# A softmax attention stage inside a two-layer encoder: order of rotation, scores, transposes and one vector's column sums

## The reference

```python
qa = partial_rotary(qa.reshape(B, L, DIFF_HEADS, 2, DIFF_QK_DIM), cos, sin)
ka = partial_rotary(ka.reshape(B, L, DIFF_HEADS, 2, DIFF_QK_DIM), cos, sin)
...
s = jnp.einsum('bqhcd,bkhcd->bhcqk', q_blk, k).astype(jnp.float32) * scale
p = jax.nn.softmax(s, axis=-1)
a = p[:, :, 0] - lam * p[:, :, 1]
return jnp.einsum('bhqk,bkhe->bqhe', a.astype(v.dtype), v)
```

## Time and profile before

| | value |
|---|---|
| median of three runs | 2928.39 us |
| runs | 2918.54, 2929.75, 2928.39 us |
| profiled execution: span from first to last instruction | 2927.6 us |
| mean granted TensorE clock over the span | 0.950 |
| PE busy | 2643.3 us (90%) |
| DVE busy | 1887.8 us (64%) |
| ACT busy | 1084.7 us (37%) |
| POOL busy | 131.7 us (4%) |
| HBM read | 613.50 MB |

### The profile page before, as it was taken

How to read it: one execution, slowest core, us unless ns; L and a number is a source line. 1 busy time by engine, 2 the same in 40 slices (tenths; PEclk the granted TensorE clock), 3 DMA queues, 4 the chain that set the end, 5 groups by cost and what they waited for, 6 DMA issues and landing times.

```text
span 2927.6 us, 43304 instructions
## 1 busy us (share of the span) xinstructions
PE 2643.3 (90%) x17226; PEld 2127.0 (73%) x17226; DVE 1887.8 (64%) x1930; ACT 1084.7 (37%) x872; POOL 131.7 (4%) x201
## 2 busy tenths in 40 slices
PE   6969999966778999999999967859979999999997
PEld 3438888832367788888888862548868888888886
DVE  7866666567645776776777757646676666555555
ACT  3333333334423333334444421123333343344442
POOL 1020000000000200000000021010020000000000
PEclk9989999987979999999999978979989999999999
DMA  7988888712423788787877759378837777555551
GB/s 251 346 275 268 282 265 278 242 54 65 145 101 129 244 281 272 258 274 264 281 262 278 278 170 225 131 197 286 298 110 236 238 233 239 187 186 186 175 185 56
DMA packets 289323, 638.99 MB, mean 218 GB/s; under 512 B 78338, under 2 KB 79364, under 8 KB 285636
## 3 DMA queue, kind: packets, MB, share of 16 engines
q1 hardware_dynamic: 239284, 583.70, 60.1%
q0 software_dynamic: 11008, 35.99, 4.2%
q10 hardware_dynamic: 38928, 17.86, 2.3%
HBM read 613.50 MB, written 19.79 MB: 216 GB/s over the span
## 4 chain that ended last, share of the span: by engine, by line
PE 78%; DVE 12%; ACT 4%; ACTq 3%; DMA 1%; issue 1%; SPq 1%; DVEq 0%
PE PS L267 46%; PE PS L268 24%; ACT Pb L967 2%; ACTq L1011 2%; DVE Pb L1747 2%; DVE acc L1742 1%; PE PS L913 1%; PE PS L184 1%; PE PS L719 1%; PE PS L220 1%; DMA omat<-WF 1%; DVE wlo L257 1%; PE PS L740 1%; ACTq L419 1%; ACT HF L967 1%
## 5 line engine op out<-in xcount | busy, mean ns | idle before, releaser
L267 PE MATMUL PS<-H,whi 128*128 128x512 f32 x5888 | 2084.2, 399 | 99.3 <-DVE wlo L257 75.5
L268 PE MATMUL PS<-H,wlo 128*128 128x256 f32 x5888 | 1656.9, 281 | 0.0
L267 PEld LDWEIGHTS PS<-H,whi 128*128 128x128 f32 x5888 | 1112.6, 189 | 371.0 <-DVE wlo L257 81.7
L257 DVE TENSOR_TENSOR wlo<-raw,whi 128x2048 fp32r<-128x2048 f32 x368 | 843.5, 2293 | 740.1 <-ACT whi L253 739.6
L253 ACT ACTIVATE whi<-raw 128x2048 fp32r<-128x2048 f32 x368 | 705.6, 1918 | 1261.0 <-PE PS L268 1227.9
L268 PEld LDWEIGHTS PS<-H,wlo 128*128 128x128 f32 x5888 | 1119.6, 190 | 0.0
L176 DVE SCALAR_TENSOR_TENSOR acc<-araw,cact,acc 128x1024 f32<-128x1024 f32 x240 | 307.1, 1280 | 1.4 <-DMA araw<-in_ada_w 0.8
L967 ACT ACTIVATE Pb<-PS 128x1024 f32 (+5 forms) x117 | 117.9, 1035 | 151.7 <-issue 59.4
L967 ACT ACTIVATE H<-Pb 128x512 fp32r (+2 forms) x142 | 94.8, 668 | 42.6 <-DVE Pb L1414 28.7
L1462 DVE TENSOR_TENSOR H<-Pb,H 128x512 fp32r<-128x512 f32 x128 | 87.6, 685 | 0.0
L1358 DVE TENSOR_TENSOR raw<-Pb,HF 128x1024 f32<-128x1024 f32 x64 | 74.1, 1220 | 9.8 <-DMA omat<-WF 7.0
(11 more groups left out here) (262 smaller groups left out, 1328.7 us busy)
## 6 DMA issues: line engine op xcount, KB each, us to landing
raw<-in_mlp_w SPq DMA_DIRECT2D x256, 1024.0 KB, 6.0
araw<-in_ada_w SPq DMA_DIRECT2D x276, 512.0 KB, 4.6
raw<-in_mix_w_in SPq DMA_DIRECT2D x64, 1024.0 KB, 7.6
raw<-in_s_w_glu SPq DMA_DIRECT2D x32, 1024.0 KB, 7.3
acc<-in_ada_w SPq DMA_DIRECT2D x44, 512.0 KB, 7.2
raw<-in_ada_w POOLq DMA_DIRECT2D x32, 512.0 KB, 4.1
raw<-in_mix_w_out SPq DMA_DIRECT2D x16, 1024.0 KB, 5.2
vmat<-Pb ACTq DMA_DIRECT2D x8, 1024.0 KB, 7.4
```

The costliest lines, as they stand in the source:

```text
L257: nc.vector.tensor_tensor(wlo[:, s % 2, :], raw[:, s, :], whi[:, s % 2, :].bitcast(F), ALU.subtract).then_inc(S("lo_done"), 1)
L267: nc.tensor.matmul(PS[:, b, :], w[0], H2[:, :, k, :], start=first, stop=False, skip_group_check=True)
L268: return nc.tensor.matmul(PS[:, b, 0:T], w[1], H2[:, 0, k, :], start=False, stop=last, skip_group_check=True)
```

## The change

The diff below is complete but for context. In words:

- Rotation groups go in the order 0, 2, 1, 3 (ROT_ORDER). Scores of heads 0 to 3 need groups 0 and 2 alone. DVE does three rotations, then `row_max(0)` and `row_max(1)`, then the fourth rotation.
- On PE the wait for all rotations and all copies ahead of the first scores is replaced by waits for the copies that free their banks (`vt_evac` 6 and 8) and for two rotations (`rot_done` 2, and 3 at turn 8). The wait for four rotations stands after scores 1.
- On ACT the three sigmoids stand ahead of all eight copies.
- `ada_sum(pe, SCALE1, 7)` moves from after scores 1 to decay level 3, behind that level's gate parts, with a wait for `lv_put` 2. `ada_finish` on DVE moves to level 5, ahead of its multiply. The turn of the gate vector at level 6 waits for it.
- GATE_WIN moves to columns 1120 to 1232 of `acc`, away from SCALE1's half.
- In the loop PE computes scores n+2 ahead of the wait for `at_mix` and the transposes.
- The masks get a semaphore of their own (`ld_mask`), and their load waits for SHIFT1 rather than SCALE1.

```diff
--- before.py
+++ after.py
@@ -198,7 +198,7 @@
     AREAS = [acc[:, 1024 * k:1024 * k + 1024] for k in range(4)] + [araw[:, k, :] for k in range(2)]
     ROWS = 3 * D // 512
     GATE_ROWS = D // 512
-    GATE_WIN = acc[:, 3072:3184].rearrange("p (k m) -> p k m", k=16)
+    GATE_WIN = acc[:, 1120:1232].rearrange("p (k m) -> p k m", k=16)
     GATE_TURN = acc[0:GATE_ROWS, 2560:3072]
     GT = acc[0:ROWS, 0:512]
 
@@ -364,6 +364,7 @@
 
 
 
+    ROT_ORDER = (0, 2, 1, 3)
     ROTW = raw[:, 3, 0:128]
     COS = raw[:, 3, 128:384]
     SIN = raw[:, 3, 384:640]
@@ -533,10 +534,10 @@
             load(ROTW, a["rot"], "ld_rot")
             load(COS, a["cos"], "ld_rot")
             load(SIN, a["sin"], "ld_rot")
-            sp.wait_ge(S(f"{SCALE1.name}_freed"), 1)
+            sp.wait_ge(S(f"{SHIFT1.name}_freed"), 1)
             for q in range(4):
                 load(acc[32 * q:32 * q + 32, 640:1120].rearrange("p (m t) -> p m t", m=15),
-                     a["masks"][:, 0:32, 0:32].rearrange("m s t -> s m t"), "ld_rot")
+                     a["masks"][:, 0:32, 0:32].rearrange("m s t -> s m t"), "ld_mask")
             sp.wait_ge(S("gate_used"), 32)
             for s in plan_out:
                 stream(s)
@@ -754,25 +755,27 @@
                                                    Pb[:, (16 if w == 0 else 48) + h, t * P:(t + 1) * P], ident[:])
                     last.then_inc(S("vt_T"), 1)
 
-                for g in range(4):
-                    if g >= 2:
-                        pe.wait_ge(S("rot_done"), g - 1)
+                for i, g in enumerate(ROT_ORDER):
+                    if i >= 2:
+                        pe.wait_ge(S("rot_done"), i - 1)
                     for z in range(2):
                         n = 2 * g + z
-                        last = nc.tensor.matmul(PS[:, 4 + 2 * (g % 2) + z, :], ROTW, PF[:, n * 512:(n + 1) * 512],
+                        last = nc.tensor.matmul(PS[:, 4 + 2 * (i % 2) + z, :], ROTW, PF[:, n * 512:(n + 1) * 512],
                                                 start=True, stop=True)
                     last.then_inc(S("rot_mm"), 1)
-                    values(0, g)
+                    values(0, i)
                 for g in range(4):
                     pe.wait_ge(S("vt_evac"), g + 1)
                     values(1, g)
-                pe.wait_ge(S("rot_done"), 4)
-                pe.wait_ge(S("vt_evac"), 8)
 
                 def scores(n):
                     h, qt = n // 2, n % 2
                     if n >= 2:
                         pe.wait_ge(S("at_exp"), n - 1)
+                    else:
+                        pe.wait_ge(S("vt_evac"), 6 + 2 * n)
+                    if n in (0, 8):
+                        pe.wait_ge(S("rot_done"), 2 + n // 4)
                     for c in range(2):
                         last = nc.tensor.matmul(PS[:, 2 * (n % 2) + c, 0:T],
                                                 Pb[64 * c:64 * c + 64, h, qt * P:(qt + 1) * P],
@@ -781,18 +784,18 @@
 
                 for n in range(2):
                     scores(n)
-                ada_sum(pe, SCALE1, 7)
+                pe.wait_ge(S("rot_done"), 4)
                 pe.wait_ge(S("win_ready"), 2)
                 nc.tensor.matmul(PS[:, 6, 0:2], ones[:, 0:P], ZERO2, start=True, stop=True, skip_group_check=True)
                 for n in range(16):
                     h, par = n // 2, n % 2
+                    if n < 14:
+                        scores(n + 2)
                     pe.wait_ge(S("at_mix"), n + 1)
                     for kt in range(2):
                         last = nc.tensor.transpose(PS[:, 4, par * T + kt * P:par * T + (kt + 1) * P],
                                                    EA[:, par, 0, kt * P:(kt + 1) * P], ident[:])
                     last.then_inc(S("at_T"), 1)
-                    if n < 14:
-                        scores(n + 2)
                     pe.wait_ge(S("at_Te"), n + 1)
                     for kt in range(2):
                         last = nc.tensor.matmul(PS[:, 5, par * T:par * T + P], Vn[:, h, kt, :], AT[:, par, kt, :],
@@ -844,7 +847,11 @@
                     if lv < 7:
                         for c in range(GATE_SPLIT[lv], GATE_SPLIT[lv + 1]):
                             gate_part(pe, c)
+                    if lv == 3:
+                        pe.wait_ge(S("lv_put"), 2)
+                        ada_sum(pe, SCALE1, 7)
                     if lv == 6:
+                        pe.wait_ge(S(f"{SCALE1.name}_freed"), 1)
                         gate_turn(pe)
                 pe.wait_ge(S("sc_ready"), 4)
                 pe.wait_ge(S("lv_put"), 7)
@@ -1098,11 +1105,10 @@
                 run(RS[n - 1], PS[0:ROWS, 0, 0:T], ACT.Sqrt, "rms_std", scale=1.0 / P, bias=eps[0:ROWS, 1:2])
 
             def attention_act():
+                run(PF[:, 8192:12288], PF[:, 8192:12288], ACT.Sigmoid)
+                run(SIGQ, QH, ACT.Sigmoid)
+                run(SIGG, GH, ACT.Sigmoid, "hg_sig")
                 for g in range(8):
-                    if g == 4:
-                        run(PF[:, 8192:12288], PF[:, 8192:12288], ACT.Sigmoid)
-                        run(SIGQ, QH, ACT.Sigmoid)
-                        run(SIGG, GH, ACT.Sigmoid, "hg_sig")
                     act.wait_ge(S("vt_T"), g + 1)
                     dst = (HF[:, 0:2048] if g < 4 else PF[:, 4096:6144])[:, 512 * (g % 4):512 * (g % 4) + 512]
                     run(dst, PS[:, g % 4, :], sem="vt_evac")
@@ -1521,13 +1527,18 @@
             v.wait_ge(S("ld_rot"), 48)
             v.wait_ge(S("in_done"), 1)
             cs, sn = (z.unsqueeze(1).broadcast_to([P, 4, T]) for z in (COS, SIN))
-            for g in range(4):
-                v.wait_ge(S("rot_mm"), g + 1)
+
+            def rotate(i):
+
+                g = ROT_ORDER[i]
+                v.wait_ge(S("rot_mm"), i + 1)
                 qk = Pb[:, 4 * g:4 * g + 4, :]
-                link(tt(ROTT, bank(4 + 2 * (g % 2), 2).rearrange("p (b t) -> p b t", b=4), sn, ALU.mult))
+                link(tt(ROTT, bank(4 + 2 * (i % 2), 2).rearrange("p (b t) -> p b t", b=4), sn, ALU.mult))
                 link(tt(qk, qk, cs, ALU.mult))
                 link(tt(qk, qk, ROTT, ALU.add))
                 v.sem_inc(S("rot_done"), 1)
+            for i in range(3):
+                rotate(i)
 
             def rms_inverse(n):
                 v.wait_ge(S("rms_std"), n)
@@ -1606,12 +1617,12 @@
                     link(tt(LN_KEY[0], LC[0], LN_KEY[0], ALU.subtract))
                 else:
                     link(tt(LN_KEY[1], LC[1], LN_KEY[1], ALU.add))
-                    v.wait_ge(S("ld_rot"), 112)
+                    v.wait_ge(S("ld_mask"), 64)
                     link(tt(acc[:, 640:864], acc[:, 640:864], acc[:, 864:1088], ALU.add))
 
             row_max(0)
             row_max(1)
-            ada_finish(v, link, SCALE1, 7)
+            rotate(3)
             link(nc.vector.memset(TINY, 1e-18))
             link(nc.vector.memset(GATE_WIN, 0.0))
             link(nc.vector.tensor_copy(GATE_WIN[:, :, GATE_ROWS - 1:GATE_ROWS].rearrange("p k m -> p (k m)"), cact[:]))
@@ -1671,6 +1682,8 @@
             for lv in range(1, 8):
                 if lv < 7:
                     level_arg(lv + 1)
+                if lv == 5:
+                    ada_finish(v, link, SCALE1, 7)
                 level_mul(lv)
                 if lv == 1:
                     level_put(1, 0, 0)
```

## The result

The changed kernel takes 2900.8 us (median of 4 runs, 2895.25 to 2905.83) against 2929.07 us (4 runs, 2918.54 to 2934.04): ratio 0.9919, 95% interval 0.9895 to 0.9944. The forecast was 2906.4 us, with a range of 2895 to 2920. The profiled execution took 2899.89 us and has a span of 2897.8 us, so 2.1 us lie around the span, not the 0.8 that I took.

What follows compares the result with a forecast made beforehand. Mostly PE products over the whole span; in this stage a serial chain before the loop, then DVE. Gains of 24.3 us less 0.3 and 2 gave 22: span 2905.6, plus 0.8 makes 2906.4 us, range 2895 to 2920.

Steps and rivals of the forecast that it cites:

- Up to `mix(0)`: Stretch before the loop: `mix(0)` starts at 604.95 instead of 617.24, 12.3 us gained, with the fourth rotation late next.
- Turns 0 and 1: First loop turns: PE's clock falls in the gap, leaving 12.0 us gained so far; 13.6 if the clock stays up.
- Turns 2 to 8: Maxima of scores 3 to 10: seven intervals, three of 4.0 and four of 4.1, 28.5 us in all; 8.2 us gained.
- Logarithms: Turn 8: the waits for ACT's logarithms stay; only the transposes no longer precede scores 12, 0.4 us gained.
- Turns 11 to 14: Late loop, called turns 11 to 13 in the forecast: DVE's full hole goes, 3 x 1.23 = 3.7 us gained.
- Levels: Decay levels: column sums hidden in PE's slack, taken as 0; DVE's addition and handshake cost 0.3 us.
- Clock in the loop: Low-clock stretches of PE in the loop, up to 3 us each for three; taken as a loss of 2 us.
- Rival 1: PE's clock oscillates through the loop, which gains nothing; only 12.3 us before it stay: 2916 us, chance 0.14.

Runs made afterwards that it cites:

- x6: Changed kernel with only ACT's three sigmoids put back behind the fourth copy: median 2911.94 us, ratio 0.9959 to the kernel before.
- x3: Changed kernel with only the scale vector's column sums put back ahead of the loop, in bank 7: median 2911.62 us, ratio 0.9973 to the kernel before.
- x5: Changed kernel with only all four rotations put back ahead of the first scores: median 2900.11 us, ratio 0.9911 to the kernel before.
- x7: Changed kernel plus six useless 128x512 products in PE's gap ahead of the loop: median 2897.79 us, ratio 0.9922 to the kernel before.
- x10: Changed kernel plus useless products in both PE gaps, six ahead of the loop, seven in turn 9: median 2901.34 us, ratio 0.9907 to the kernel before.
- x1: The changed kernel timed again with no edit: median 2897.21 us against 2920.16 for the kernel before, ratio 0.9923.
- x4: Changed kernel with the column sums ahead of the loop in bank 4, free after the third rotation: median 2907.31 us, ratio 0.9947 to the kernel before.

## Why the prediction was right or wrong

- *Up to `mix(0)`:* 12.3 us forecast, 12.2 measured (33.97 - 21.77). The fourth rotation was late next, as forecast. The share of each edit is another than its size suggests. Undone one by one, and counted from DVE's first rotation, the sigmoids are worth 9.0 us, the column sums 7.3, the order of rotations and scores 0. The first two make 16.3 and not 12.2 because each was undone in the new order: there the fourth rotation comes behind the late sigmoids (x6), under which it ran before, and the sums in bank 7 wait for it (x3). With all rotations first, x5 beside the kernel before, the first scores come at 18.04 instead of 23.92 us, and `mix(0)` 3.53 instead of 10.05 us behind them: 5.9 us of the sigmoids and 6.5 of the sums.
- *Turns 0 and 1:* 12.0 forecast at the fourth maximum, 12.0 measured, with the clock fallen in the gap as I took it. Had it stayed up, x7 gives 2.8 us more, where I had 1.6.
- *Turns 2 to 8:* 28.5 us forecast for seven intervals, 29.39 measured (59.43 - 30.04). PE's 4.0 us is right to 0.1 (4.05 and 4.15 in the short turns); DVE's turn with four L1568 is 4.26, not 4.1. 7.3 us instead of 8.2.
- *Logarithms:* 0.4 forecast, 1.1 measured (16.96 - 15.88). With the loop's new order and one gate part a turn, this interval lies at 15.9 to 16.3 us or at 17.1 to 17.2, and at 14.5 with the gap filled (x10): the low clock behind the gap adds 1.4 to 2.7 us to it.
- *Turns 11 to 14, up to the maxima of scores 15:* 3.7 forecast, 3.26 measured (17.87 against 14.61).
- *Levels:* -0.3 forecast, -0.2 measured (83.66 against 83.89); the sums were hidden as forecast, in 3.73 us.
- *Clock in the loop,* the one term that failed in kind: "I take -2 us". The granted clock was 1.00 from 614 to 650, and nothing was lost. Rival 1, and with it the rule from the Trainium skill ("TensorE: Matmul & The Clock Gate", "A second HAM failure mode: psum-queue depth-cycling"), didn't come about in the turns with a gate part each; the measurement decides. The trace of before had more low stretches, and with more idle time in a turn.
- *Not in the sum:* 1.0 us behind level 7 (42.46 against 41.47), where the sums of the norm on PE (L473 before) took 5.33 us instead of 6.17 by a later fall of the clock. Nothing in the change does that.

Forecast for the stretch 22 us, measured 24.5: 2.0 more for the clock that didn't fall in the loop, 1.0 more behind level 7, and 0.5 less from the other terms, whose errors (-0.9, +0.7, -0.4, +0.1) happen to cancel in part. The medians moved by 28.3 in the first set and 23.0 in x1, on both sides of it. The range held the time, though the scatter of the medians is larger than the terms that were argued over. What wasn't seen ahead is that the first of the listed edits, the scores after two of four groups, does nothing: the sum had it inside the 12.3 without a price of its own.

## What to carry to other kernels

Ahead of a loop, add up what each engine must do before its first turn: an edit that only reorders work of the engine that paces it gains nothing, while moving another engine's work out of the chain gained all of it here, with either of two idle places for the column sums. What such an edit is worth depends on the order of the rest: the fourth rotation cost nothing while it ran under the sigmoids. In a loop over three engines, let the next turn's first product be issued before the wait for this turn's result, and check that the in-order engine's full turn (4.0 us here) isn't then longer than the pacing engine's (3.6 to 4.5). Judge changes of half a per cent at fixed points of the trace: here the untouched rest scattered by 24 us, while the stage repeated to 0.3 in the one kernel traced twice. Then look whether the first point itself is clean: in four of thirteen traces 1.4 to 1.6 us that looked like an effect lay in the first two products.

## What was not expected of the hardware

A gap on PE costs twice. In turn 9 PE is idle for 6.92 us while the granted clock falls to 0.63 and then 0.52; its next product takes 1.22 us instead of 0.71 and the gate part 2.75 to 3.58 instead of 1.88. With products of no use in the gap DVE's wait for scores 12 fell by 1.4 to 2.7 us (x10). The clock also fell in shorter gaps: behind 3.94 us of column sums and 2.25 us idle in x4, and ahead of scores 0 after 3.62 us idle in x5. It doesn't fall each time: behind the same 2.62 us of idle time ahead of the rotations it stayed up in nine traces and was low in four. Gains of 1 to 3 us made early in such a stage are given back or doubled by where the later low stretches fall (x7: 2.9 us at the fourth maximum, 0 at the output projection; x4: 0.3 lost at `mix(0)`, 3.6 at the output projection). One such place can be read from the rows: in x4 the gate parts of level 5 ran at full clock and were done sooner, so PE waited 2.20 us for level 6 instead of 0.62, and level 6 took 2.82 us instead of 2.09. There a fast piece lengthened the gap behind it, and the next piece ran slow.
